# A hybrid encoder step on one core: combination ahead of the maxima, row steps moved, first loads in the constants' block, last row tile in column halves

## The reference

```python
y_a = rg_lru(causal_conv(a_x)) * silu(a_g)            # width 512
y_b = dsa(q, k, v, top-256 keys by the indexer) * silu(b_g)   # 4 heads of 64
p = softmax(mask(s))                                   # C: two maps for each of 4 heads
attn = p[:, :, 0] - lam * p[:, :, 1]
o = rmsnorm(attn @ v, subln) * (1 - lam_init)          # C, then * silu(c_g)
x = x + rmsnorm(concat(y_a, y_b, y_c) @ w_out, norm_post)
```

## Time and profile before

| what | us |
|---|---|
| median of three runs | 1707.88 |
| profiled execution | 1700.6 |
| its span (first to last instruction) | 1698.8 |
| TensorE busy | 1579.7 (93%) |
| VectorE busy | 1135.0 (67%) |
| ScalarE busy | 629.6 (37%) |
| GpSimd busy | 429.1 (25%) |
| stores of 512 KB to y, from issue to landing (median) | 2.9 |
| mean granted TensorE clock | 0.975 of full speed |

### The profile page before, as it was taken

How to read it: one execution, slowest core, us unless ns; L and a number is a source line. 1 busy time by engine, 2 the same in 40 slices (tenths; PEclk the granted TensorE clock), 3 DMA queues, 4 the chain that set the end, 5 groups by cost and what they waited for, 6 DMA issues and landing times. The chain is left out here.

```text
span 1698.8 us, 21027 instructions
## 1 busy us (share of the span) xinstructions
PE 1579.7 (93%) x7298; PEld 1085.2 (64%) x7298; DVE 1135.0 (67%) x2456; ACT 629.6 (37%) x1227; POOL 429.1 (25%) x540
## 2 busy tenths in 40 slices
PE   6999999999979798989989999999998888999887
PEld 4566566678867665666556666666887767466663
DVE  3478999967955645555345899999487455455551
ACT  3276621218043323433316753212452333233340
POOL 2000620530012244431410043233100212445311
PEclk9999999999989999999999999999999798999999
DMA  5100000321050212111411000113101303111101
GB/s 176 54 22 20 34 25 27 115 70 51 0 184 7 112 32 63 44 38 32 158 56 54 25 25 25 50 56 100 56 26 58 130 9 112 45 50 56 50 12 52
DMA packets 38888, 98.13 MB, mean 58 GB/s; under 512 B 8640, under 2 KB 27584, under 8 KB 34432
## 3 DMA queue, kind: packets, MB, share of 16 engines
q1 hardware_dynamic: 38784, 96.80, 17.2%
HBM read 65.79 MB, written 18.14 MB: 49 GB/s over the span
## 5 line engine op out<-in xcount | busy, mean ns | idle before, releaser
L1697 PE MATMUL ps<-r_xn,r_w 128*128 128x384 f32 (+1 forms) x1728 | 555.6, 473 | 11.8 <-DVE r_xn L1353 6.3
L1697 PEld LDWEIGHTS ps<-r_xn,r_w 128*128 128x128 f32 x1728 | 326.4, 191 | 195.3 <-issue 14.6
L1454 DVE TENSOR_SCALAR_CACHE_REDUCE r_ix<-r_sc,smi 128x768 bf16<-128x768 f32 (+6 forms) x380 | 342.0, 962 | 2.2
L1255 ACT ACTIVATE r_sc<-ps,sm 128x1024 f32<-128x1024 f32 (+8 forms) x204 | 156.1, 765 | 305.8 <-DVE sm L1588 305.4
L1588 DVE TENSOR_REDUCE sm<-ps 128x1 f32<-128x1024 f32 (+8 forms) x204 | 159.7, 786 | 120.3 <-PE ps L1856 55.6
L1773 PE MATMUL ps<-r_w,r_xn 128*128 128x256 f32 x1024 | 223.4, 380 | 0.0
L1773 PEld LDWEIGHTS ps<-r_w,r_xn 128*128 128x128 f32 x1024 | 194.1, 190 | 27.1 <-issue 1.0
L1893 PEld LDWEIGHTS ps<-r_vg,r_w 128*128 128x128 f32 (+1 forms) x1176 | 156.1, 201 | 56.7 <-issue 25.8
L1874 PE MATMUL ps<-ident,r_sc 128*128 128x128 f32 (+1 forms) x684 | 120.4, 287 | 62.6 <-DVE r_sc L641 47.5
L1874 PEld LDWEIGHTS ps<-ident,r_sc 128*128 128x128 f32 (+1 forms) x684 | 85.2, 150 | 133.8 <-issue 102.4
L1893 PE MATMUL ps<-r_vg,r_w 128*128 128x64 f32 (+1 forms) x1176 | 157.4, 280 | 7.5 <-DVE r_w L657 4.9
(11 more groups left out here) (254 smaller groups left out, 2057.3 us busy)
## 6 DMA issues: line engine op xcount, KB each, us to landing
r_w<-w_in SPq DMA_DIRECT2D x28, 1024.0 KB, 5.0
r_xn<-w_out SPq DMA_DIRECT2D x2, 4096.0 KB, 13.4
y<-r_res SPq DMA_DIRECT2D x16, 512.0 KB, 2.9
r_vg<-x SPq DMA_DIRECT2D x8, 512.0 KB, 10.0
r_xn<-ckT SPq DMA_DIRECT2D x2, 2048.0 KB, 8.5
r_xn<-vcache SPq DMA_DIRECT2D x2, 2048.0 KB, 14.2
o_v<-r_vg SPq DMA_DIRECT2D x4, 1024.0 KB, 10.9
r_sc<-x SPq DMA_DIRECT2D x8, 512.0 KB, 4.8
```

What stands on the lines that cost most here:

```text
L1255: ins = nc.scalar.activation(ex[2 * (i % 2) + m][0:r, 0:w], on_slot(("qk", i, m), w, r), ACT.Exp, bias=negm[0:r, c:c + 1], accum_out=den[0 ...
L1454: ins = vec.tensor_scalar(unsel[t][0:rows(t), :], sc[t][0:rows(t), :], b, None, op, ALU.add, accum_out=cnt[0:rows(t), c:c + 1])
L1697: ins = nc.tensor.matmul(on_ring(key, cn), w[:, k, P * s:P * (s + 1)], xnT[:, k, c0:c0 + cn], start=(k == 0), stop=(k == KT - 1))
```

## The change

Three things are changed. In `schedule()` the order of the steps is changed in the units of prompt tiles: in C units of wide tiles `own` stands first, and both exponentials follow the first transpose group; `rows_now` stands later in all of them. The first loads are issued by SP in the block that makes the constants. The last row tile of the program is squared, scaled, added and stored in two halves of 512 columns, the first half's addition on GpSimd and the second's on VectorE.

```diff
--- before.py
+++ after.py
@@ -185,7 +185,7 @@
         plain = t == SAMPLE or kind == "B"
         if len(groups) == 1:
             head = one[:-1] + ytr + one[-1:] + own if plain else own + one[:-1] + ytr + one[-1:]
-            steps += head + take(i, 1) + pv + rows_now + two + take(i, quota - 1) + groups + div
+            steps += head + take(i, 1) + pv + two + take(i, quota - 1) + groups + div + rows_now
         elif t == SAMPLE:
             ahead = []
             if i + 2 < len(units) and maps_of(i + 1) == maps_of(i + 2) == 1:
@@ -197,9 +197,12 @@
                 steps += groups[:1] + ahead[:1] + groups[1:2] + pv + groups[2:] + ahead[1:] + div
             else:
                 steps += groups[:1] + two[-1:] + pv + groups[1:] + div
+        elif plain:
+            steps += one[:-1] + ytr + one[-1:] + own + take(i, 1) + groups[:1] + two + rows_now
+            steps += take(i, quota - 1) + pv + div + groups[1:]
         else:
-            steps += one[:-1] + ytr + one[-1:] + own + rows_now + two[:-1]
-            steps += take(i, 1) + groups[:1] + two[-1:] + take(i, quota - 1) + pv + div + groups[1:]
+            steps += own + one[:-1] + ytr + two[:-1] + take(i, 1) + groups[:1] + rows_now + one[-1:] + two[-1:]
+            steps += take(i, quota - 1) + pv + div + groups[1:]
     last = len(units)
     hold[0] = last
     steps += [("pv", last - 1), ("div", last - 1)]
@@ -482,6 +485,7 @@
         sso_ready, rso_ready, res_ready = sem("sso_ready"), sem("rso_ready"), sem("res_ready")
         xres_in, half_out = sem("xres_in"), sem("half_out")
         cst_next, w_next = sem("cst_next"), sem("w_next")
+        end_filled, end_scaled, end_ready = sem("end_filled"), sem("end_scaled"), sem("end_ready")
         carry_sso, carry_rso, carry_mix = sem("carry_sso"), sem("carry_rso"), sem("carry_mix")
         carry_res, carry_stored = sem("carry_res"), sem("carry_stored")
         kc_in, wo_in, gpost_in = sem("kc_in"), sem("wo_in"), sem("gpost_in")
@@ -493,6 +497,18 @@
 
 
         with nc.Block() as block:
+            @block.sync
+            def _(sp):
+
+                for t in range(NT):
+                    r0 = P * t
+                    sp.dma_start(xt[t][0:rows(t), :], x0[r0:r0 + rows(t), :]).then_inc(x_in[t], 16)
+                    if t == 1:
+                        sp.dma_start(cst[:, :], acst[0]).then_inc(cst_in, 16)
+                    if t == 2:
+                        sp.dma_start(ring[0], w_in[0, 0]).then_inc(w_ready[0], 16)
+                sp.dma_start(ring[1], w_in[0, 1]).then_inc(w_ready[1], 16)
+
             @block.vector
             def _(dve):
 
@@ -675,15 +691,12 @@
             x_from = y if layer else x0
             has_prev, has_next = layer > 0, layer + 1 < DEPTH
             base = 1 if has_prev else NT
+            ended = None if has_next else ("rows", NT - 1)
             deferred = [("square", NT - 1), ("rows", NT - 1)] if has_next else []
             with nc.Block() as block:
 
                 @block.sync
                 def _(sp):
-                    def load_x(t):
-                        r0 = P * t
-                        sp.dma_start(xt[t][0:rows(t), :], x_from[r0:r0 + rows(t), :]).then_inc(x_in[t], 16)
-
                     def load_next(t):
                         r0 = P * t
                         sp.dma_start(xt[t][0:rows(t), :], y[r0:r0 + rows(t), :]).then_inc(x_in[t], 16)
@@ -698,15 +711,6 @@
                         r0 = P * LATE
                         sp.wait_ge(carry_res, 1)
                         sp.dma_start(y[r0:r0 + P, :], res[:, :]).then_inc(carry_stored, 16)
-                    else:
-                        load_x(0)
-                        sp.dma_start(cst[:, :], acst[layer]).then_inc(cst_in, 16)
-                        load_x(1)
-                        load_x(2)
-                        load_unit(0)
-                        for t in range(3, NT):
-                            load_x(t)
-                        load_unit(1)
                     for g in range(4):
                         sp.dma_start(ikc[DI * g:DI * (g + 1), :], kidxT[layer]).then_inc(ikc_in, 16)
                     sp.wait_ge(wg_zero, 1)
@@ -807,6 +811,13 @@
                             sp.wait_ge(o_filled, last + 1)
                             sp.dma_start(wo, w_out[layer]).then_inc(wo_in, 16)
                         elif s[0] == "rows" and s not in deferred:
+                            if s == ended:
+                                r0 = P * LATE
+                                sp.wait_ge(res_ready, NT)
+                                sp.dma_start(y[r0:r0 + P, 0:BANK], res[:, 0:BANK]).then_inc(y_stored, 16)
+                                sp.wait_ge(end_ready, 1)
+                                sp.dma_start(y[r0:r0 + P, BANK:DM], res[:, BANK:DM]).then_inc(y_stored, 16)
+                                continue
                             store(s[1])
                             if s[1] + 1 < NT:
                                 finish(s[1] + 1)
@@ -824,7 +835,7 @@
                         sp.wait_ge(w_next, 16)
                         sp.wait_ge(cst_next, 16)
                         sp.wait_ge(xres_in, 16 * NT)
-                    sp.wait_ge(y_stored, 16 * (NT - len(deferred) // 2))
+                    sp.wait_ge(y_stored, 16 * (NT - len(deferred) // 2 + (0 if has_next else 1)))
                     sp.wait_ge(stored, 16 * 6)
                     sp.wait_ge(ik_stored, 16)
 
@@ -1027,7 +1038,7 @@
                             r = rows(ORDER[n])
                             b = n % 2
                             pool.wait_ge(sso_ready, n + 1)
-                            if ORDER[n] == SAMPLE:
+                            if ORDER[n] == SAMPLE or (n == NT - 1 and not has_next):
                                 link(nc.gpsimd.tensor_tensor(sso[0:r, b:b + 1], sso[0:r, b:b + 1], sso2[0:r, :], ALU.add))
                             link(nc.gpsimd.tensor_scalar(rso[0:r, b:b + 1], sso[0:r, b:b + 1], 1.0 / DM, EPS,
                                                          ALU.mult, ALU.add))
@@ -1036,6 +1047,12 @@
                         elif s[0] == "rows":
                             n = s[1]
                             r = rows(ORDER[n])
+                            if s == ended:
+                                pool.wait_ge(end_scaled, 1)
+                                pool.wait_ge(xres_in, 16 * NT)
+                                nc.gpsimd.tensor_tensor(res[:, 0:BANK], res[:, 0:BANK], xres[:, 0:BANK], ALU.add)\
+                                  .then_inc(res_ready, 1)
+                                continue
                             pool.wait_ge(mix_drained, n + 1)
                             pool.wait_ge(xres_in, 16 * (n + 1))
                             nc.gpsimd.tensor_tensor(res[0:r, :], res[0:r, :], xres[0:r, :], ALU.add)\
@@ -1283,12 +1300,22 @@
                         elif s[0] == "square":
                             n = s[1]
                             r = rows(ORDER[n])
-                            act.wait_ge(mix_filled, n + 1)
+                            halves = n == NT - 1 and not has_next
+                            if not halves:
+                                act.wait_ge(mix_filled, n + 1)
                             mixb = mixbs[mix_place(n)]
                             if n >= 1:
                                 act.wait_ge(sso_ready, n)
                             if n >= 2:
                                 act.wait_ge(rso_ready, n - 1)
+                            if halves:
+                                act.wait_ge(end_filled, 1)
+                                nc.scalar.activation(mixsq2[:, 0, :], mixb[:, 0, :], ACT.Square,
+                                                     accum_out=sso2[:, :])
+                                act.wait_ge(mix_filled, n + 1)
+                                nc.scalar.activation(mixsq2[:, 1, :], mixb[:, 1, :], ACT.Square,
+                                                     accum_out=sso[:, n % 2:n % 2 + 1]).then_inc(sso_ready, 1)
+                                continue
 
                             if ORDER[n] == SAMPLE:
 
@@ -1607,6 +1634,16 @@
                                 dve.wait_ge(gpost_in, 16)
                             else:
                                 dve.wait_ge(y_stored, 16 * n)
+                            if s == ended:
+                                scale = rso[:, n % 2:n % 2 + 1]
+                                vec.scalar_tensor_tensor(res2[:, 0, :], mixb[:, 0, :], scale, gpost2[:, 0, :],
+                                                         ALU.mult, ALU.mult).then_inc(end_scaled, 1)
+                                link(vec.scalar_tensor_tensor(res2[:, 1, :], mixb[:, 1, :], scale, gpost2[:, 1, :],
+                                                              ALU.mult, ALU.mult))
+                                dve.wait_ge(xres_in, 16 * NT)
```

(5 more changed lines are left out.)

## The result

| | median us | range | runs |
|---|---|---|---|
| before | 1710.5 | 1705.3 to 1718.5 | 4 |
| after | 1636.5 | 1633.4 to 1637.5 | 4 |

The ratio is 0.956, with a 95% interval of 0.952 to 0.960: the change takes 74 us off. The profiled execution after took 1637.05 us, 63.5 less than the one before.

The account below looks back on a forecast made before the run. TensorE, hardly ever free, was taken as the bound, so only its idle time, clock and the program's ends could give. 32.5 + 5 + 1.5 + 1.1 + 8 = 48 off 1700.6 gave 1652.5; with 7.3 for the median, 1660, range 1638 to 1684.

Parts of the forecast that it names:

- terms 1 to 4: The four gains forecast apart from the clock: 32.5 + 5 + 1.5 + 1.1 us.
- 5. Clock: TensorE's low clock level, counted in layer 2's tiles 6 and 7: 8 of 12.5 us given back, bounds 0 and 18.
- Combination order: Combination ahead of the maxima in wide tiles' C units: cuts TensorE's 47.5 us of waits by 32.5, bounds 20 and 47.5.
- Row steps: Row step later in narrow tiles and wide B units: 4.9 + 5.6 - 4.0 (new tile 3 wait) = 6.5; 5 us taken.
- The 5.6 for the copies in tiles 4 and 5: Row step no longer ahead of the copy the second transpose group waits for: 1.40 us each, 5.6 in all.
- First loads: First loads issued in the constants' block: first projection 1.0 us earlier, with clock 1.5 taken, bounds -1.3 and 3.3.
- last tile: Last row tile in halves: second store issued 1.0 us sooner, stores landing no sooner; 1.1 us in sum, between -0.3 and 2.2.
- (b): Rival: the whole 47.5 us of combination waits goes and the clock is full; 71 us gained, 1637; chance 0.15.
- (a): Rival: clock stays as it is and the loop binds in all wide tiles; 25 us gained, 1683; chance 0.2.
- (c): Rival: no effect, second exponential ends as late as before and gaps only change name; ends alone, 1705; chance 0.04.
- (d): Rival: slower, the loop exceeds the old unit in tiles 6 and 7, each of 32 units loses; 1732; chance 0.03.
- the loop: Wide C units' cycle through VectorE and ScalarE (copy, two exponentials, combination): 5.4 us in tile 6, 5.8 in tile 7.

Follow-up runs that it names:

- comb_only: Kernel before with only the new order of combination, copy and maxima in C units of wide tiles: 1652.5 us against 1707.3.
- comb_67: Kernel before with the new C-unit order in tiles 6 and 7 alone: 1663.0 us, ratio 0.975.
- ends_only: Kernel before with only the first loads and the last row tile changed, old step order kept: 1701.3 us, ratio 0.997.
- combined: Changed kernel with tile 3's row step put back, output weights in two loads and fewer loads in the first block: 1624.1 us beside 1632.1.
- short_first: Changed kernel with only three row tiles, the constants and the first weight unit loaded in the first block: 1634.5 us, ratio 0.957.

## Why the prediction was wrong

The direction was right and so was the mechanism of the waits: terms 1 to 4, 40.1 us in sum, came to 38.3 at full clock. The size failed in one term, "5. Clock".

**Combination order, 32.5.** Right: 32.1 at full clock in comb_only. The unit in tile 6 came out at 5.2 instead of 5.4, in tile 7 at 5.55 instead of 5.8, because the two exponentials stand 1.00 apart, not the 1.1 to 1.2 that I had estimated: ScalarE's accumulator read costs the next exponential no time. The wait that stays is 11.8 where I had named about 15, in tiles 7 and 6 but for 1.0 us in all, as said.

**Row steps, 5.** Near: 3.4 at full clock. The forecast wait at tile 3 is there, 3.6 in both layers for the 4.0 that I worked out, and the 4.9 for divisions went. The 5.6 for the copies in tiles 4 and 5 was too much. The 1.40 at 763.08 went down to 0.20, but the next group of transposes now waits 1.59 (at 740.36 in the trace after), so that only 1.9 is gained in both layers. The prediction had feared that POOL's addition might fall on something else, and it does. Beside this addition, which runs from 737.67 to 740.01, a step of VectorE's division that takes 0.23 us elsewhere takes 2.27, and the copy stands behind it:

```profile
737.82 2.27 DVE L687 SCALAR_TENSOR_TENSOR r_w<-r_w 128x64 f32<-128x64 f32 x1
```

**First loads, 1.5, and last tile, 1.1.** Right in most parts: second block at 7.35 (7.9), transposes at 11.56 (12.1), first projection at 18.62 (19.2), last store issued 2.67 behind VectorE's start (2.7). Together 4.5 at full clock instead of 2.6. Wrong was that "the stores land no sooner": the halves landed in 2.1 us, and the end of the span moved up by 1.0 for it. I had read the size off the sample tile's stores, 256 KB in 3.0 us, which are 64 rows of 4 KB where a half of the last tile is 128 rows of 2 KB. No run shows whether that makes the difference. The section of the Trainium skill that the prediction cites here ("DMA: Bandwidth & Descriptors", anatomy of one DMA) is about DMAs issued by GpSimd, and these come from SP; its 0.6 us is an estimate for another path, but nearer to the measured 0.8 to 1.1 than my nothing. The first 16 projections at full clock (1.7 us, of which I had counted 0.5) are low time and not in the 4.5; right behind them, from 24 to 40 us, the granted clock is 0.89, so part of it only moved.

**A wait that I had not seen.** 3.8 us for the load of the output weights, 2.7 of it in layer 2. It comes with the combination's new order (comb_only has 2.7 over both layers): the load of 4 MB takes 13.8 us from its issue, which stands behind the sample tile's last value products (1359.82 in layer 2), and TensorE's first projection step, in tile 6, now comes sooner (1374.70, 2.7 of it waited). Asking what comes late next would have found it; the prediction asked that of the row steps, not of the weights.

**Clock, 8, with a bound of 18.** This is the step that failed. Measured: low time from 90.6 to 22.1 us, which at 0.50 is 34. The rate was right (0.45 from the earlier trace rows against 0.50). The amount was wrong, in two ways, with a small third:

1. I counted the low time of two stretches, tiles 7 and 6 of layer 2, 28 us of it. The execution had 78, visible in the granted clock of most stretches: 14 in layer 1's tile 7 and sample tile, 16 in the narrow tiles of both layers. The upper bound should have been 0.50 times all of it, 39.
2. I took 8 of 12.5 because "what gaps remain is half of what was". Waits go by such a share. The clock did not: 42 of the 49 us of low time in the stretches of tile 7, the sample tile and tile 6 went when gaps of 2 us became gaps of 1 us, and comb_67 shows that the order in these two tiles is enough for it.
3. I carried the 7.3 us between the profiled execution and the median over to the forecast, as if it were something the change leaves alone. By the line under 3 of it is low time (84.9 in the profiled execution against 90.6 in the mean), which goes with the gaps. The other 5 are the distance of that execution from the line, for which I have no cause; they are why the profiled pair shows 63.5 of the 74.

Layer 1's tile 6, which kept 1.00 with the same gaps that went with 0.76 in layer 2, misled me into weighing the clock down. Other executions differ there: ends_only, with the same gaps in that stretch, has 0.91 in it:

```profile
560.00:620.00 60.00, 51.52 (x309) 40.31 (x309) 33.66 (x85) 20.46 (x46) 16.95 (x27) 0.91 0.23 84
```

One execution's clock is a sample of what those gaps do.

The Trainium skill ("TensorE: Matmul & The Clock Gate", Part 1, on a second failure mode) tells of a kernel in which TensorE "micro-idles between MM groups frequently enough" that the clock swings between its levels (there in cycling through PSUM banks), and the same part says that activity releases the throttle. The runs agree with both, and more strongly than I had allowed: with repeated waits of 2 us, none over 3.2, 91 us of 1700 were at 1.2 GHz, and filling the waits with useless matmuls halved that.

**Rivals.** (b), the whole wait and a full clock, gave 1637 and the time is 1636.5, but not for its reasons: it takes 43 from the combination order (though it speaks of the whole 47.5) and 16 from the clock, and the runs show 32 and 34. Its number came out by luck, two errors that cancel. (a), (c) and (d) fell: the loop binds in tiles 7 and 6 alone, and below my estimate.

**What stays open.** Why tiles 4 and 5, with as many but shorter gaps, cost no clock: their gaps (0.7 to 1.3 us) and the work between them both differ from tiles 6 and 7, and no run tells the two apart. The clock's own rule stays unknown with it: the runs show what closing the gaps gave back, not what length or share of idle time lowers the level. And of the three single edits in combined, runs on one chip show the sum (8.0) but not the shares.

## What to carry to other kernels

When a trace shows granted clock below 1.00 beside short, repeated waits of TensorE, sum the low time over the whole span (twice the missing share of each stretch) and price each microsecond of it at half a microsecond, the price of this kernel, before anything else; that sum is the bound of what closing the gaps can give on top of the waits, and the difference between two executions of one kernel may be the same thing. Filling the gaps with useless transposes is a cheap test of it that changes no dependency. And when a unit becomes shorter, go through the loads that were timed against the old one: a 13.8 us load that had always been in time was late by 2.7.

## What the hardware showed that I had not expected

- Twelve useless transposes in each of 14 units made the program 19 us faster (1688.2 against 1707.3).
- The run-to-run spread of this kernel, 18 us, follows the granted clock with 0.50 us per us at the low level (89% of the variance in 32 runs).
- At the start, the same 16 projections took 5.40 us in four profiled executions with a gap of 1.36 to 1.72 us ahead of them, 6.86 to 7.09 in three with 1.81 or 1.82, 7.09 in combined with 2.62, and 8.46 in short_first with 3.18. These are single executions; that the gap is the cause isn't shown.
- Two stores of 256 KB landed in 2.1 us where one of 512 KB took 3.2.
- VectorE's addition of 512 columns beside POOL's took 1.20 us, against 0.74 for its scaling of the same width just before, and 0.75 on average for another instruction of this width with two inputs in SBUF (L1443, 14 times). The Trainium skill ("GPSIMD Engine Reference", Key points) names this: the two share their interfaces to SBUF, with contention for VectorE instructions that have two SBUF inputs. The trace agrees: the addition has two, the scaling one and a PSUM bank. No run has the addition without POOL's beside it, but three other VectorE instructions show the same: they took 1.69 us (at 763.25 before), 2.27 (737.82 after) and 2.46. All four ended 0.1 to 0.6 us behind POOL's addition.
